# Output projection of a mixer layer: two plain token tiles and eight pairs in place of four and seven, with all sums of weight blocks on VectorE

## What is computed

```python
m = g_a * (y_a @ w_proj_a) + g_b * (y_b @ w_proj_b)
z = x + gate * (m @ w_out)          # w_out: 1024 x 1024
y = z * rsqrt(mean(z * z) + EPS) * final_g
```

## Time and profile before

| | us |
|---|---|
| median of 3 runs (1723.14 to 1723.63) | 1723.22 |
| the profiled execution, its own time | 1724.99 |
| its span, first to last instruction | 1723.4 |
| PE busy in the span | 1701.1 (99%) |
| DVE busy | 1242.2 (72%) |
| ACT busy | 862.1 (50%) |
| GpSimd busy | 653.6 (38%) |

### The profile page before, as it was taken

One profiled execution on the slowest core, in us unless ns is written; L12 is line 12 of the kernel. 1 busy time (PEld: TensorE's weight loads), 2 busy tenths in 40 slices (PEclk: granted clock), 3 DMA queues, 4 the chain that ended last, 5 costly groups with the idle time before them and its releaser, 6 DMA issues.

```text
span 1723.4 us, 27674 instructions
## 1 busy us (share of the span) xinstructions
PE 1701.1 (99%) x9909; PEld 1442.6 (84%) x9909; DVE 1242.2 (72%) x1789; ACT 862.1 (50%) x1501; POOL 653.6 (38%) x509
## 2 busy tenths in 40 slices
PE   8999999999999999999999999999999999999998
PEld 5787888888899988888888888889898888888886
DVE  3785888788757858888687856777777665677776
ACT  3553434455567644434544437777779222333443
POOL 0044675565200026856555653224223100005443
PEclk9999999999999999999999999999999999999999
DMA  9443534333598734444333368988666777673442
GB/s 325 126 150 126 135 124 143 93 92 110 178 309 262 211 96 129 155 132 111 98 127 100 104 172 219 230 205 209 167 146 172 247 231 234 191 261 134 148 158 86
DMA packets 271644, 286.31 MB, mean 166 GB/s; under 512 B 49960, under 2 KB 217748, under 8 KB 268309
## 3 DMA queue, kind: packets, MB, share of 16 engines
q1 hardware_dynamic: 271106, 284.18, 56.0%
q10 hardware_dynamic: 403, 0.37, 0.1%
HBM read 203.18 MB, written 81.30 MB: 165 GB/s over the span
## 4 chain that ended last, share of the span: by engine, by line
PE 86%; DMA 4%; DVE 3%; issue 2%; POOL 2%; ACT 1%; SPq 1%; POOLq 0%; ACTq 0%; DVEq 0%
PE banks L1837 38%; PE banks L2391 6%; PE banks L2965 4%; PE banks L2967 4%; PE banks L2966 4%; DMA w_raw<-in_w_in 3%; PE banks L3025 3%; PE banks L3027 3%; PE banks L3026 3%; PE banks L2355 2%; PE banks L1967 2%; PE banks L1966 2%; PE banks L1965 2%; PE banks L2361 2%; PE banks L2331 1%
## 5 line engine op out<-in xcount | busy, mean ns | idle before, releaser
L1837 PE MATMUL banks<-a_hi,w_hi 128*128 128x512 f32 x1176 | 460.2, 391 | 0.8 <-ACT out_stage L1117 0.4
L1837 PE MATMUL banks<-a_hi,w_lo 128*128 128x512 f32 x1176 | 457.8, 389 | 0.0
L1837 PE MATMUL banks<-a_lo,w_hi 128*128 128x512 f32 x1176 | 457.7, 389 | 0.0
L1506 DVE SCALAR_TENSOR_TENSOR banks<-glu_out,taps,banks 128x1009 f32<-128x1009 f32 (+1 forms) x240 | 342.2, 1426 | 5.2
L1837 PEld LDWEIGHTS banks<-a_hi,w_hi 128*128 128x128 f32 x1176 | 220.8, 188 | 50.0 <-issue 3.6
L1837 PEld LDWEIGHTS banks<-a_hi,w_lo 128*128 128x128 f32 x1176 | 220.8, 188 | 46.4
L1837 PEld LDWEIGHTS banks<-a_lo,w_hi 128*128 128x128 f32 x1176 | 220.9, 188 | 45.0
L1006 POOL TENSOR_TENSOR t_raw<-w_raw 128x512 f32<-128x512 f32 x39 | 53.6, 1373 | 400.6 <-DMA w_raw<-in_w_in 394.4
L1425 DVE SCALAR_TENSOR_TENSOR w_lo<-w_raw,w_hi 128x1024 fp32r<-128x1024 f32 x84 | 108.9, 1296 | 104.9 <-ACT w_hi L1097 103.6
L960 POOL TENSOR_TENSOR w_lo<-t_raw,w_hi 128x1024 fp32r<-128x1024 f32 x70 | 171.6, 2461 | 23.7 <-ACT w_hi L1097 21.4
L2503 ACT ACTIVATE probs<-scores,stat 128x640 f32<-128x640 f32 (+2 forms) x128 | 106.6, 833 | 51.2 <-DVE stat L2425 49.8
(11 more groups left out here) (282 smaller groups left out, 3678.6 us busy)
## 6 DMA issues: line engine op xcount, KB each, us to landing
w_raw<-in_w_in SPq DMA_DIRECT2D x34, 1024.0 KB, 5.7
cw_raw<-in_w_in SPq DMA_DIRECT2D x44, 512.0 KB, 5.0
proj<-out_stage SPq DMA_DIRECT2D x80, 256.0 KB, 2.3
gates_in<-proj SPq DMA_DIRECT2D x64, 256.0 KB, 3.0
k_hi<-k_hi_rows SPq DMA_DIRECT2D x16, 640.0 KB, 11.5
k_lo<-k_lo_rows SPq DMA_DIRECT2D x16, 640.0 KB, 13.5
q_split<-q_rows SPq DMA_DIRECT2D x8, 1152.0 KB, 6.0
w_ada<-in_w_ada SPq DMA_DIRECT2D x8, 1024.0 KB, 11.2
```

The source lines that it names most:

```text
L1506: op = dve.scalar_tensor_tensor(dst, src, by, dst, ALU.mult, ALU.add)
L1837: op = pe.matmul(out, x[w][:, b, k], y, start=(start and k == j == 0), stop=(k == H - 1 and j == 2), skip_group_check=not start)
```

## The change

- Two plain tiles, 14 and 15, and eight pairs: tiles 0 and 1, 2 and 3, up to 12 and 13, and last 16 and 17. Four plain units in place of eight; the plain banks are 6, 7, 2 and 3, so that the first pair's banks need not be waited for.
- Since tiles 16 and 17 are now a pair, chunk 4's last two tiles are stored to memory: eight stores of 128x256 more. `load_m_pair` for the first two pairs waits for all five chunks' stores. On SP, the loads of B11, B12, x and B22 stand between the last stores, and B21's load stands behind the load of the first pair.
- All four weight sums are on DVE, in the order T1, T3, unit 0, T2, T4, unit 1; GpSimd makes only token sums and rms factors.
- The lists of ACT, DVE and GpSimd for the first pair are written in another order. The three final scalings ahead of the pairs are gone; final(0) and final(1) stand in the first pair, behind C22 and C12.
- In the first pair `sum_22` stands ahead of the next pair's S1 and A12 low parts, and ACT's `copy_first` ahead of the S4 and A22 high parts.
- The low parts of the weights go in the order T1, T2, T3, T4. The second pair's m is loaded once three plain units are done.

```diff
-OUT_BANKS = [6, 7, 4, 5, 0, 1, 2, 3]
-OUT_TILES = list(range(14, NTOK)) + list(range(14))
-PLAIN = 4
+OUT_BANKS = [6, 7, 2, 3]
+OUT_TILES = [14, 15] + list(range(14)) + [16, 17]
+PLAIN = 2
...
-T_HIGHS, T_LOWS = ["T1", "T3", "T2", "T4"], ["T1", "T3", "T2", "T4"]
-POOL_SUMS = [("T2", 0), ("T4", 0)] + [(s, e) for e in range(NE) for s in ("S1", "S2", "S3", "S4")]
+T_HIGHS, T_LOWS = ["T1", "T3", "T2", "T4"], ["T1", "T2", "T3", "T4"]
+POOL_SUMS = [(s, e) for e in range(NE) for s in ("S1", "S2", "S3", "S4")]
...
     def store_m(sp, og):
...
+        first = P * PLAIN if c == 4 else 0
         sp.wait_ge(m_done, og + 1)
-        sp.dma_start(io.m[P * o:P * o + P, col:col + w], m_raw[:, og % MR, 0:w]).then_inc(m_out[og % MR], 16)
+        sp.dma_start(io.m[P * o:P * o + P, col + first:col + w], m_raw[:, og % MR, first:w]).then_inc(m_out[og % MR], 16)
...
-                sp.wait_ge(m_out[r], m_base[r] + 16 * 8 // MR * 4)
+                sp.wait_ge(m_out[r], m_base[r] + 16 * 8 // MR * 5)
...
         sp.wait_ge(m_lod, 8)
         load_m_pair(sp, 0)
+        load_block(sp, "B21")
         load_x(sp, 4)
+        sp.wait_ge(mm2, 3)
+        load_m_pair(sp, 1)
         for p in range(NTOK - 1):
-            if p == PLAIN - 1:
-                sp.wait_ge(mm2, 7)
-                load_m_pair(sp, 1)
...
-        if name == "P5" and e == 0:
-            pe.wait_ge(z_done, 4)
...
-        square_unit(act, 6)
-        square_unit(act, 7)
+        square_unit(act, 2)
+        square_unit(act, 3)
+        copy_first(act, 0)
+        token_high(act, "S4", 0)
         token_high(act, "A22", 0)
...
-                if MR <= og < 32 + MR:
+                if og >= MR:
                     dve.wait_ge(m_out[og % MR], m_base[og % MR] + 16 * (og // MR))
...
             finish_part("C11", e)
+            if e == 0:
+                sum_22(e)
             if more:
                 token_low(dve, "S1", e + 1)
                 token_low(dve, "A12", e + 1)
-            sum_22(e)
+            if e:
+                sum_22(e)
             finish_part("C22", e)
+            if e == 0:
+                final(0)
             sum_12(e)
             finish_part("C12", e)
+            if e == 0:
+                final(1)
             if more:
                 finish_part("C21", e)
...
         pool.wait_ge(summed, s_base + 2)
-        block_sum(pool, "T2", pool_sum)
+        token_sum(pool, "S1", 0)
+        token_sum(pool, "S2", 0)
+        token_sum(pool, "S3", 0)
         rms_of(0)
-        pool.wait_ge(pool_sum, POOL_SUM_AT["T2", 0])
-        block_sum(pool, "T4", pool_sum)
-        token_sum(pool, "S1", 0)
+        token_sum(pool, "S4", 0)
         rms_of(1)
```

More of the change, by code:

```diff
@@ L2686, in tail @@
     t_hi, t_lo, s_raw = {}, {}, {}
-    for n, where in (("A11", X_AT + 16384), ("S1", ln_at), ("S2", X_AT + 20480), ("A12", ln_at + 4096), ("S3", X_AT + 24576),
-                     ("S4", ln_at + 8192), ("A22", X_AT + 28672)):
+    for n, where in (("A11", X_AT + 24576), ("S1", X_AT + 28672), ("S2", X_AT + 16384), ("A12", ln_at + 8192), ("S3", ln_at),
+                     ("S4", X_AT + 20480), ("A22", ln_at + 4096)):
         t_hi[n], t_lo[n] = at(f"mo_{n}_hi", [P, H, P], where, F32R), at(f"mo_{n}_lo", [P, H, P], where + 2048, F32R)
@@ L2861, in tail_sync @@
                 load_x(sp, 0)
[L2862 to L2874, removed]
+            if og == 38:
+                sp.wait_ge(mm, 76)
+                sp.wait_ge(wo_hid, 4)
+                load_block(sp, "B11")
+                load_block(sp, "B12")
+                sp.wait_ge(g_done, 76)
+                load_x(sp, 1)
+            if og == 39:
+                sp.wait_ge(g_done, 78)
+                load_x(sp, 2)
+                sp.wait_ge(mm, 80)
+                load_block(sp, "B22")
+            store_m(sp, og)
         sp.wait_ge(g_done, 80)
@@ L3096, in block_high @@
     def block_high(act, n):
[L3097 to L3100, removed]
+        act.wait_ge(summed, s_base + T_HIGHS.index(n) + 1)
         act.activation(bhi[n], t_raw[n], ACT.Copy).then_inc(wo_hid, 1)
@@ L3105, in slot_free @@
         name = next(p for p, a, _ in BLOCK_PRODUCTS if a == n)
-        eng.wait_ge(mm2, OM_AT[name, e - 1] if e else 2 * SLOT_TILE[n] + 2)
+        if e:
+            eng.wait_ge(mm2, OM_AT[name, e - 1])
+        elif n in SLOT_TILE:
+            eng.wait_ge(mm2, 2 * SLOT_TILE[n] + 2)
     def m_block(n, e):
@@ L3127, in copy_first @@
         act.wait_ge(mm2, OM_AT["P1", e])
-        act.wait_ge(z_done, Z_AT["C11", e - 1] if e else 3)
+        if e:
+            act.wait_ge(z_done, Z_AT["C11", e - 1])
         act.activation(c11_at, sums_at[e % 2], ACT.Copy).then_inc(copied, 1)
@@ L3138, in copy_second @@
         act.wait_ge(mm2, OM_AT["P6", e])
-        act.wait_ge(z_done, Z_AT["C12", e - 1] if e else 5)
+        if e:
+            act.wait_ge(z_done, Z_AT["C12", e - 1])
         act.activation(c12_at, sums_at[e % 2], ACT.Copy).then_inc(copied, 1)
@@ L3324, in block_low @@
         if n in ("T1", "T2"):
[L3325 removed]
+            dve.wait_ge(summed, s_base + T_HIGHS.index("T2" if n == "T1" else "T4") + 1)
         dve.tensor_tensor(blo[n], t_raw[n], bhi[n].bitcast(F32), ALU.subtract).then_inc(wo_lod, 1)
@@ L3422, in sum_12 @@
             dve.tensor_tensor(c12_at, c12_at, s1t1[:], ALU.add).then_inc(summed, 1)
-        block_sum(dve, "T1", summed)
+        block_sum(dve, "T1")
+        block_sum(dve, "T3")
         unit(0)
-        block_sum(dve, "T3", summed)
+        block_sum(dve, "T2")
+        block_sum(dve, "T4")
         unit(1)
         block_low(dve, "T1")
-        block_low(dve, "T3")
-        unit(2)
-        final(0)
-        unit(3)
-        block_low(dve, "T2")
-        block_low(dve, "T4")
-        unit(4)
-        final(1)
-        token_low(dve, "A11", 0)
-        token_low(dve, "S1", 0)
-        unit(5)
-        token_low(dve, "A12", 0)
-        final(2)
-        unit(6)
-        token_low(dve, "S2", 0)
+        token_low(dve, "A11", 0)
+        unit(2)
+        token_low(dve, "S1", 0)
+        block_low(dve, "T2")
+        unit(3)
+        token_low(dve, "A12", 0)
+        token_low(dve, "S2", 0)
+        block_low(dve, "T3")
         token_low(dve, "S3", 0)
         token_low(dve, "S4", 0)
-        unit(7)
+        block_low(dve, "T4")
         token_low(dve, "A22", 0)
@@ L3456, in tail_dve @@
                 final(PLAIN + 2 * e - 2)
-            final(PLAIN + 2 * e - 1)
+                final(PLAIN + 2 * e - 1)
             finish_part("C11", e)
+            if e == 0:
+                sum_22(e)
             if more:
```

47 lines of the change are left out of this document (21 added, 26 removed).

## The result

| | before | after |
|---|---|---|
| median of 21 runs each, us | 1723.28 | 1725.96 |
| lowest to highest | 1722.24 to 1727.55 | 1722.46 to 1729.74 |
| ratio, 95% interval | | 1.0013 (1.0007 to 1.0018) |
| span of the profiled execution | 1723.4 | 1724.1 |

The change costs 0.13%, some 2.2 us by the ratio, where +1.7 us was forecast; it is inside the 0.2% that I had called no change (the interval lies above 1, so it is a cost, if a small one). 12 matmuls are gone, and more than that has come back as waits of PE.

What follows compares the result with a forecast made beforehand. PE, busy throughout the output projection, was taken as the bound. Removed work of -2.84 us plus stalls of 1.7, 0.5, 1.4 and 0.9 gave +1.7 on the median 1723.22: 1724.9 us, range 1720.6 to 1727.4.

Steps and rivals of the forecast that it cites:

- Removed: -2.84: On PE, four plain units (22.00 us) become one pair (19.16), 12 matmuls fewer: -2.84 us.
- The loads: On SP's queue, counted from 1500: m_pair0 lands at 49.5; B21, issued at 44.4 behind it, lands 7.4 later, at 51.8.
- my walk: DVE's list step by step, counted from 1500: T4's sum waits for B21 and GpSimd, running 52.2 to 54.4.
- P1 of pair 1: First pair's start on PE, 59.65 counted from 1500: its preparation has 1 us to spare, no stall.
- P6 of pair 1: First pair on PE: waits for ACT's first copy and DVE's S2 low, starting at 66.8, not 65.1; stall 1.7 us.
- P7 of pair 1: First pair on PE: waits for ACT's third copy, behind GpSimd's rms and token sum; stall 0.5 us.
- P6, P7 and P4 of pair 2: Second pair on PE: stalls 1.4 (ACT's square and copy), 0 (m_pair2's landing) and 0.9 us (DVE's sum_22).
- The sum: All terms together: -2.84 + 1.7 + 0.5 + 1.4 + 0.9 = +1.7 us, giving 1724.9; chance of this case 0.50.
- Rival 1: The cover mostly suffices: stalls shrink to 1.4 us, net -1.4, 1721.8; chance 0.30 for stalls 0 to 3.
- Rival 2: GpSimd shut out by DVE at first pair's P7, stalling 3.6: net +4.2, 1727.4; with later landings, chance 0.20.
- the four places named for gaps: PE gaps expected in the profile after: ahead of P6 and P7 of the first pair, P6 and P4 of the second.
- two of the signs that I had named: Stated signs of error: B21 landing past 1553, a PE gap at P1 or P5, or later pairs waiting.

Runs made afterwards that it cites:

- e3: Changed kernel with B21's load behind the last m store, m_pair2's ahead of tile 0's store, second pair's ACT copy ahead of the square; projection 175.31 us, ratios 0.9987, 0.9985.
- after3: The changed kernel run a third time, unchanged, with B21 landing early; projection 178.54 us, ratio to before 1.0002.
- e5: Changed kernel with ACT's copy of P1 put ahead of the square of C21 in the second pair; projection 181.06 us, ratio to before 1.0011.
- e2: Changed kernel with m_pair2 loaded ahead of the store of tile 0 and the load of x behind it; projection 176.32 us, ratio to before 1.0003.
- after2: The changed kernel run again, unchanged, with B21 landing late; projection 180.56 us, ratio to before 1.0008.
- e6: Changed kernel with the first pair's copy_first and sum_22 back in the order of all other pairs; projection 179.85 us, ratio to before 1.0018.
- e7_poolsums: Changed kernel with weight sums T2 and T4 back on GpSimd, ahead of its token sums; projection 182.82 us, ratio to before 1.0023.

## Why the prediction was right, and where it wasn't

**Removed: -2.84.** Exact. It is the length of e3 in both executions.

**The loads.** m_pair0 was issued 6.78 behind the projection's start and landed by 12.1; I had 6.15 and 11.85. B21 was issued at 7.2 (I had 6.75) and landed 8.8 later, not 7.4: T4's sum began at 16.04 against the 14.55 of my walk. The 7.4 was right for three of seven executions. I took it from one row, that of B12, and should have given the range of such a load's landing.

**P1 of pair 1: no stall, in fact 0.57.** T4's sum began 1.49 later than I had it, and I had 1 us to spare.

**P6 of pair 1: 1.7, in fact 1.77.** A right number by two errors that cancel. From T4's start to P6 I walked 14.6; the rows give 13.94 (1551.37 to 1565.31), because GpSimd's S4 sum met S1 low for 0.6 (its row has 1.29 in place of 0.68), not 1.2. With T4 at my 14.55 the gap would be about 1.0; with after3's 13.44 it is none.

**P7 of pair 1: 0.5, in fact none of note** (a distance of 0.34 at 1571.04). The walk through rms_of and S1 was right in kind. The third copy ended at 1570.89, 0.15 ahead of P7. Counted from the projection's start it came 0.5 later than I had it, but P6 had started 0.83 later (29.98 against 29.15), and that moved P7's need by as much.

**P6, P7 and P4 of pair 2: 1.4, 0 and 0.9, in fact 1.01, 1.00 and 0.73.** Sum 2.3 against 2.74. The mis-sized term is P7's, put at 0. I had m_pair2 issued at 46.95 behind the projection's start and landing in 6.1; it was issued at 47.6 and took 6.7, with tile 1's store behind it. And since P6's stall was smaller than I had it, P7 wanted to start earlier, and the fixed landing took back what P6 had not lost. e5 shows that exchange. SP's wait behind final(0) and a landing store is what I had described, and e2 shows it.

**Restarts.** Each gap also lengthens the next distances by about 0.1. I had not counted that; with the other long distances it is 0.85 in all.

**The sum.** +1.7 forecast; +3.1 and +2.4 in the two executions with a late B21, +0.4 in the one with an early B21, +2.2 by the ratio. That the forecast lies among these is in part luck. The stalls of after are 5.93 with the long distances, where I had 4.5; P1 of pair 1 and P7 of pair 2, put at 0, had 0.57 and 1.00, the 0.5 at P7 of pair 1 wasn't there, and P6's number came of two errors. The mechanism held: the late transfers and the copies and sums behind them. Rival 1 (1721.8) is half true of an early landing: with it the first pair has no gap, as it says, but the second pair's remain. Its argument against itself, 2.9 us of idle time ahead of T4, is 3.1 by my own walk (48.7 to 51.8), and was 3.84. Rival 2 (shut out at P7) didn't happen. GpSimd's z_var did wait, 2.63 us (a DVE low part and the weight low part that followed), and its z_rstd for 0.29; the token sum then got in between two low parts, and its copy came in time:

```profile
1556.38 1.55 POOL L3499 TENSOR_SCALAR z_var<-z_ssum 128x1 f32<-128x1 f32 x1 [4.82 <-ACT z_square L3152]
...
1564.78 2.63 POOL L3499 TENSOR_SCALAR z_var<-z_ssum 128x1 f32<-128x1 f32 x1 [4.94 <-ACT z_square L3152]
...
1567.49 0.85 POOL L3501 TENSOR_TENSOR z_rstd<-z_var,z_half 128x1 f32<-128x1 f32 x1
...
1568.32 1.36 POOL L3344 TENSOR_TENSOR mo_S_raw<-m_pair 128x512 f32<-128x512 f32 x1
```

By the Trainium skill, "SBUF — State Buffer", "SBUF: two separate sides", whichever starts first has the ports for the whole instruction. The 2.63 is longer than that: z_var was asked for at 1564.78, inside the S2 low part (1564.44 to 1565.13), and came only behind the T3 low part (to 1567.32). The row decides: a short GpSimd instruction may have to wait for the DVE instruction that runs and for the next one. The first z_var shows the same: asked for inside the T1 low part (to 1557.25), it ended at 1557.93, behind the A11 low part (to 1557.85). And the 2.63 comes again, to the hundredth, in after2, after3, e2, e5 and e6. The 1.36 of the token sum agrees with the page.

**In the list of what would show it:** the plain and pair matmuls are as forecast, the four places named for gaps had P7 of pair 1 too many and P1 of pair 1 and P7 of pair 2 too few, and pairs 3 to 8 are free of gaps. By two of the signs that I had named I was wrong: PE has a gap at P1, and B21 landed past 1553 as the prediction counts (16.0 behind the projection's start, where 1553 is 15.4). The time came out inside the range all the same, because the margin at P1 took up most of the delay and S4's sum cost 0.6 less.

## What to carry to other kernels

Less work on the bounding engine pays only as far as the cover that it gave isn't needed: list what was prepared under it, and walk that list engine by engine with the loads in their new order on the queue. A transfer belongs where its issuer would otherwise stand waiting, ahead of a store and its landing and not behind; here two such moves and one copy turned +2.2 us (over three sets of runs +0.3 to +2.2) into about -2.4. And price a transfer by a range of landings: a margin smaller than that range is a gap in some executions.

## What the runs showed of the hardware

- The same 1 MB load, issued at the same place in the same order, landed 7.4 or 7.5 us behind its issue in three executions and 8.8 to 9.2 in four. B22's load and the last store of m were slower in the same four, m_pair0's load was not. What decides isn't shown; the chip alone doesn't.
- The projection's first matmul started between 1534.88 and 1538.43 in executions whose programs don't differ up to the last chunk of the merge: 3.5 us of spread, more than the effect under study. The length of the stage, not the span, told the kernels apart.
- Behind a gap of PE the first one or two distances of matmuls are 0.30 to 0.34 us in place of 0.23, at a granted clock of 1.00.
- In e7_poolsums, behind gaps of 0.88 and 2.44 us, the granted clock was 0.50 for some 3 us, with matmuls 0.43 us apart. No gap of the other executions, up to 1.78 us, was followed by that.
